# Attention scores: one four-byte matmul against three passes over rounded parts, and one bias load per head against eight

## The reference

```python
s = jnp.einsum('brqhd,brakhd->bhrqak', qg, kg,
               preferred_element_type=jnp.float32) * (d ** -0.5)
bias = rpb[:, dr[:, None, :, None], dc[None, :, None, :]]
s = s + bias[None].astype(jnp.float32)
s = jnp.where(col_in[None, None, None, :, None, :], s, -jnp.inf)
p = jax.nn.softmax(s.reshape(B, H, rows, GRID_W, kr * GRID_W), axis=-1).reshape(s.shape)
o = jnp.einsum('bhrqak,brakhd->brqhd', p.astype(v.dtype), vg)
```

## Time and profile before

| | |
|---|---|
| time, median of 3 runs | 2923.58 us (2922.88 to 2926.93) |
| the profiled execution | 2923.64 us, span from first to last instruction 2922.1 us |
| TensorE busy | 95% of the span |
| VectorE, ScalarE, GpSimd busy | 55%, 45%, 13% |
| mean granted TensorE clock | 0.981 of full speed |

### The profile page before, as it was taken

The page is one execution under the profiler, slowest core; times in us unless marked ns, Lnnn a source line. Parts: engine busy times, 40 slices in busy tenths (PEclk is TensorE's granted clock), DMA queues, the critical chain, the costliest instruction groups (busy, mean ns, idle before and its releaser), DMA issues.

```text
span 2922.1 us, 33578 instructions
## 1 busy us (share of the span) xinstructions
PE 2778.2 (95%) x12738; PEld 2280.3 (78%) x12738; DVE 1599.1 (55%) x1769; ACT 1325.6 (45%) x1459; POOL 388.6 (13%) x603
## 2 busy tenths in 40 slices
PE   8999999999999999989999966999999999999993
PEld 7888888888888887768777745888888888888882
DVE  4111111321333236675234647888888888888885
ACT  6111111211111115654232324777777777777774
POOL 1200000020110033571010101000000000000002
PEclk9999999999999999999999987999999999999996
DMA  8322112121332247534353557999999999999997
GB/s 317 89 79 79 65 57 79 58 100 50 106 103 101 86 146 221 183 105 143 125 173 128 166 172 284 379 401 403 390 400 407 402 404 404 404 400 406 400 394 277
DMA packets 193952, 663.74 MB, mean 227 GB/s; under 512 B 24073, under 2 KB 49176, under 8 KB 170656
## 3 DMA queue, kind: packets, MB, share of 16 engines
q1 hardware_dynamic: 169088, 564.52, 51.3%
q0 software_dynamic: 24736, 97.54, 10.0%
HBM read 588.09 MB, written 73.83 MB: 227 GB/s over the span
## 4 chain that ended last, share of the span: by engine, by line
PE 90%; DMA 2%; DVE 2%; POOL 2%; issue 2%; ACT 1%; SPq 0%; POOLq 0%; DVEq 0%; ACTq 0%
PE ps L2178 24%; PE ps L1877 18%; PE ps L1855 6%; PE ps L1856 6%; PE ps L1857 6%; PE ps L2118 4%; PE ps L2120 4%; PE ps L2119 4%; PE ps L2201 4%; PE ps L2200 4%; PE ps L2199 4%; PE ps L1940 1%; PE ps L1920 1%; PE ps L2157 1%; PE ps L2082 1%
## 5 line engine op out<-in xcount | busy, mean ns | idle before, releaser
L1764 DVE TENSOR_TENSOR elo<-eraw,ehi 128x2048 fp32r<-128x2048 f32 x384 | 874.5, 2292 | 137.0 <-ACT ehi L1223 130.3
L1223 ACT ACTIVATE ehi<-eraw 128x2048 fp32r<-128x2048 f32 x384 | 733.3, 1920 | 250.2 <-PE ps L2178 163.7
L1307 DVE TENSOR_TENSOR wlo<-raw,whi 128x1024 fp32r<-128x1024 f32 x96 | 117.6, 1225 | 705.5 <-ACT whi L969 705.5
L969 ACT ACTIVATE whi<-raw 128x1024 fp32r<-128x1024 f32 x96 | 101.7, 1059 | 733.2 <-PE ps L1877 393.3
L2178 PE MATMUL ps<-elo,xh 128*128 128x512 f32 x960 | 373.8, 389 | 0.0
L2178 PE MATMUL ps<-ehi,xh 128*128 128x512 f32 x960 | 373.7, 389 | 0.0
L1855 PE MATMUL ps<-whi,a_hi 128*128 128x512 f32 x768 | 300.2, 391 | 10.1 <-DVE a_lo L1317 10.1
L1856 PE MATMUL ps<-wlo,a_hi 128*128 128x512 f32 x768 | 300.0, 391 | 0.0
L1857 PE MATMUL ps<-whi,a_lo 128*128 128x512 f32 x768 | 300.0, 391 | 0.0
L2178 PE MATMUL ps<-ehi,xl 128*128 128x512 f32 x960 | 256.7, 389 | 0.0
L1877 PE MATMUL ps<-a_hi,whi 128*128 128x512 f32 x768 | 236.9, 390 | 1.8 <-DVE t L1339 1.6
(11 more groups left out here) (264 smaller groups left out, 3920.4 us busy)
## 6 DMA issues: line engine op xcount, KB each, us to landing
eraw<-in_w_gate SPq DMA_DIRECT2D x256, 512.0 KB, 6.1
eraw<-in_w_up SPq DMA_DIRECT2D x256, 512.0 KB, 8.3
eraw<-in_w_down SPq DMA_DIRECT2D x128, 1024.0 KB, 10.6
raw<-in_w_stream SPq DMA_DIRECT2D x96, 512.0 KB, 3.5
oraw<-in_w_stream SPq DMA_DIRECT2D x128, 256.0 KB, 2.6
scr_rows<-stage POOLq DMA_DIRECT2D x48, 256.0 KB, 2.3
scr_feats<-stage POOLq DMA_DIRECT2D x44, 256.0 KB, 2.3
t<-in_xT SPq DMA_DIRECT2D x16, 512.0 KB, 5.7
```

What stands on the lines that cost most here:

```text
L1223: act.activation(ehi[:, p % ERING, :], flat2(eraw[:, 2 * (p % EDEEP):2 * (p % EDEEP) + 2, :]), ACT.Copy)\
L1764: dve.tensor_tensor(elo[:, p % ERING, :], flat2(eraw[:, 2 * (p % EDEEP):2 * (p % EDEEP) + 2, :]), ehi[:, p % ERING, :].bitcast(F32), ALU.s ...
```

## The change

The scores are made like the projection: ScalarE copies each head's `naq` and `nak` (128x1024 each) into rounded parts, VectorE subtracts these in place, which leaves the remainders where `naq` and `nak` were, and `qk` is three fp32r matmuls of 384 columns into one bank. The copies and subtractions of head `h + 1` stand in the lists of ScalarE (iterations 1 and 2 of head `h`) and VectorE (iterations 2 and 3); those of head 0 stand in the last projection block. `qk` waits for the second remainder (`na_lo`) where it waited for the transfer. Beside it, GpSimd writes a second scratch tensor `rpb_skew` with 8 DMAs from `rpb_rep`, once, behind the store of projection block 7, and `fetch_skew` becomes one DMA of 384 KB.

```diff
             def fetch_skew(h):
 
-                for r in range(QR):
-                    row = h * 15 + 7 - r
-                    sp.dma_start(skew[r * QC:(r + 1) * QC, h % 2, :, :], t["rpb_rep"][:, row:row + 16, :]).then_inc(nbsem[h % 2], 16)
+                sp.dma_start(skew[:, h % 2, :, :], t["rpb_skew"][:, h * 15:h * 15 + 16, :]).then_inc(nbsem[h % 2], 16)
...
+            pool.wait_ge(S["rep_out"], 16 * QC)
+            for r in range(QR):
+                pool.dma_start(t["rpb_skew"][r * QC:(r + 1) * QC, :, :], t["rpb_rep"][:, QR - 1 - r:P - r, :]).then_inc(S["rep_out"], 16)
...
+            def query_high(h):
+
+                hb = h % 2
+                act.wait_ge(nqsem[hb], 32 * (h // 2) + 32)
+                if h >= 2:
+                    act.wait_ge(S["qk_done"], 8 * (h - 1))
+                act.activation(naq_hi[hb][:, :], naq[:, hb, :], ACT.Copy).then_inc(S["na_hi"], 1)
+
+            def key_high(h):
+
+                act.activation(nak_hi[h % 2][:, :], nak[:, h % 2, :], ACT.Copy).then_inc(S["na_hi"], 1)
...
                 evict_pt(v)
                 if v + NAD < NAU:
                     expo(v + NAD)
+                if v % 8 == 1 and v + 8 < NAU:
+                    query_high(v // 8 + 1)
+                if v % 8 == 2 and v + 8 < NAU:
+                    key_high(v // 8 + 1)
...
+            def query_low(h):
+
+                hb = h % 2
+                dve.wait_ge(S["na_hi"], 2 * h + 1)
+                dve.tensor_tensor(naq_lo[hb][:, :], naq[:, hb, :], naq_hi[hb][:, :].bitcast(F32), ALU.subtract).then_inc(S["na_lo"], 1)
...
                 if v:
                     finish(v - 1)
+                if v % 8 == 2 and v + 8 < NAU:
+                    query_low(v // 8 + 1)
+                if v % 8 == 3 and v + 8 < NAU:
+                    key_low(v // 8 + 1)
...
                 if u == 0:
-                    pe.wait_ge(nqsem[hb], 32 * (h // 2) + 32)
+                    pe.wait_ge(S["na_lo"], 2 * h + 2)
...
-                pe.matmul(score_bank(v), q, k, start=True, stop=True).then_inc(S["qk_done"], 1)
+                pe.matmul(score_bank(v), q_hi, k_hi, start=True, stop=False)
+                pe.matmul(score_bank(v), q_hi, k_lo, start=False, stop=False)
+                pe.matmul(score_bank(v), q_lo, k_hi, start=False, stop=True).then_inc(S["qk_done"], 1)
```

More of the change, by code:

```diff
@@ L166, in trunk, with place_split @@
         stage_end, = place(19456, ("stage_end", [P, 4, BW]))
+        def place_split(at, *names):
+            stack = ExitStack()
+            stack.enter_context(nc.sbuf_tensor("below_" + names[0], [P, (at - ROOM) // 4], F32))
+            made = [stack.enter_context(nc.sbuf_tensor(name, [P, SEQ], F32R)) for name in names]
+            stack.close()
+            return made
+        nq0_lo, nq1_lo, nk0_lo, nk1_lo = place_split(126464, "nq0_lo", "nq1_lo", "nk0_lo", "nk1_lo")
+        nq0_hi, nk0_hi = place_split(216576, "nq0_hi", "nk0_hi")
+        nq1_hi, nk1_hi = place_split(118336, "nq1_hi") + place_split(55296, "nk1_hi")
+        naq_lo, nak_lo, naq_hi, nak_hi = (nq0_lo, nq1_lo), (nk0_lo, nk1_lo), (nq0_hi, nq1_hi), (nk0_hi, nk1_hi)
         mv0, mv1, mbc0, kn1, wexp, kw, qkw = place(
@@ L254, in trunk @@
                   "c_updated hs_done ones_done gate_act gate_arg gate_out "
-                  "gates_in h_out0 g_sum wr_in").split():
+                  "gates_in h_out0 g_sum wr_in na_hi na_lo").split():
             S[n] = sem(n)
@@ L268, in trunk @@
         REDO = NE - 2
-        ER0 = [32 * BLK + 16 * OHB * KD // RING] * RING + [32 * (NAH // 2)] * 2 + [256 * (NAH // 2)] * 2 + [128 * (NAH // 2)] * 2
+        ER0 = [32 * BLK + 16 * OHB * KD // RING] * RING + [32 * (NAH // 2)] * 2 + [256 * (NAH // 2)] * 2 + [16 * (NAH // 2)] * 2
         def rows_landed(eng, T):
@@ L509, in fetch_ml_o @@
                 sp.dma_start(mo[h % 2][:, :, :], row_tiles(2048 + h * DV, 2048 + (h + 1) * DV)).then_inc(mosem[h % 2], 16)
-            sp.wait_ge(S["rep_out"], 16 * QC)
+            sp.wait_ge(S["rep_out"], 16 * (QC + QR))
             sp.wait_ge(S["w_used"], 7 * (BLK - 1) + 4)
@@ L768, in _ @@
                 mask_tile(y)
-            pool.wait_ge(nbsem[0], 128)
+            pool.wait_ge(nbsem[0], 16)
             pool.wait_ge(S["nmask_done"], 6)
@@ L786, in _ @@
             for h in range(1, NAH):
-                pool.wait_ge(nbsem[h % 2], 128 * (h // 2 + 1))
+                pool.wait_ge(nbsem[h % 2], 16 * (h // 2 + 1))
                 if h >= 2:
@@ L1037, in _ @@
             feats_high(BLK - 1, True)
+            def query_high(h):
[6 more added lines that the diff above has]
+                act.activation(nak_hi[h % 2][:, :], nak[:, h % 2, :], ACT.Copy).then_inc(S["na_hi"], 1)
+            query_high(0)
+            key_high(0)
             def misc_bank(h, j):
@@ L1450, in feats_low, with key_low @@
                         low(b + 1, m)
+                else:
+                    query_low(0)
+                    key_low(0)
                 evict_feats(b)
+            def query_low(h):
+                hb = h % 2
+                dve.wait_ge(S["na_hi"], 2 * h + 1)
+                dve.tensor_tensor(naq_lo[hb][:, :], naq[:, hb, :], naq_hi[hb][:, :].bitcast(F32), ALU.subtract).then_inc(S["na_lo"], 1)
+            def key_low(h):
+                hb = h % 2
+                dve.wait_ge(S["na_hi"], 2 * h + 2)
+                dve.tensor_tensor(nak_lo[hb][:, :], nak[:, hb, :], nak_hi[hb][:, :].bitcast(F32), ALU.subtract).then_inc(S["na_lo"], 1)
             for b in range(ROWBLK + 2, BLK):
@@ L1914, in qk @@
                 if u == 0:
-                    pe.wait_ge(nqsem[hb], 32 * (h // 2) + 32)
+                    pe.wait_ge(S["na_lo"], 2 * h + 2)
                 if v >= NAD:
                     pe.wait_ge(S["scored"], v - NAD + 1)
-                q = naq[:, hb, u * P:(u + 1) * P]
-                k = nak[:, hb, :].rearrange("p (r c) -> p r c", c=GW)[:, 4 * r:4 * r + WR, KCOL[c]:KCOL[c] + WC]
-                pe.matmul(score_bank(v), q, k, start=True, stop=True).then_inc(S["qk_done"], 1)
+                q_hi, q_lo = (a[hb][:, u * P:(u + 1) * P] for a in (naq_hi, naq_lo))
+                k_hi, k_lo = (a[hb][:, :].rearrange("p (r c) -> p r c", c=GW)[:, 4 * r:4 * r + WR, KCOL[c]:KCOL[c] + WC]
+                              for a in (nak_hi, nak_lo))
+                pe.matmul(score_bank(v), q_hi, k_hi, start=True, stop=False)
+                pe.matmul(score_bank(v), q_hi, k_lo, start=False, stop=False)
+                pe.matmul(score_bank(v), q_lo, k_hi, start=False, stop=True).then_inc(S["qk_done"], 1)
             def tr(v):
@@ L2229 @@
     "m_rows": (8, SEQ), "decays": (8, TT), "q_rows": (2, P, SEQ),
-    "rpb_rep": (QC, P, 48), "h2": (SEQ, D),
+    "rpb_rep": (QC, P, 48), "rpb_skew": (P, P - QR + 1, 48), "h2": (SEQ, D),
 }
```

## The result

| | before | after |
|---|---|---|
| time, median of 7 runs | 2923.58 us (2921.9 to 2926.93) | 2935.03 us (2933.61 to 2937.2) |
| span of the profiled execution | 2922.1 us | 2934.2 us |
| mean granted TensorE clock | 0.981 | 0.980 |

The change makes the kernel slower by 11.4 us: ratio 1.0037, interval 1.0026 to 1.0047. I forecast 2925.4 and no measurable change. The time lies at the upper end of the range, where the rival "slower by transfers" (2934.4) stood.

What follows compares the result with a forecast made beforehand. TensorE was taken to bound an attention iteration of 1.64 us. Passes -7.8, splits +7.0 and transfers +2.6 summed to +1.8 us on 2923.64, giving 2925.4 us, range 2917 to 2935, no measurable change (0.48).

Steps and rivals of the forecast that it cites:

- slower by transfers: Rival: mLSTM bytes land as late as before, heads 5, 6, 7 wait 5.3, 3, 4.5 us, clock falls; 2934.4 us, chance 0.26.
- three passes: Scores on TensorE: three matmuls of 0.173 make 0.52 us instead of 0.65, gaining 7.8 us over 59 iterations.
- splits: Copies on ScalarE and subtractions on VectorE stall TensorE 1.0 us per head, 7.0 us lost over seven heads.
- transfers: Attention stage: `nak` needed four iterations sooner; waits and clock cost 9.2 us against 6.6 now, 2.6 us lost.
- Slower by the passes: Rival: a 384-column matmul on TensorE costs 0.2266 us as 512 columns do; 2932.1 us, chance 0.07.
- The third stall of 0.4: Per head: second subtraction ends late, score and exponential follow late, and `evict_pt` misses its `pv` by about 0.4 us.
- VectorE two subtractions of 1.23 us: Split step: for heads 1 to 7 VectorE gets two subtractions per head of 1.23 us each.
- the 0.7 that I took off for the shorter SyncE list: Head 5's `nak`: landing taken at 1146.5, where the bound by the bytes was 1147.2.
- less 3 us for skew: Head 7's `nak`: the merged skew load brings its landing 3 us sooner, to 1177.3, leaving a wait of 2.4 us.
- The clock: Behind head 5's wait of 4.5 us TensorE's clock falls to its lower level, charged at 1.3 us.
- The rest cost nothing: Head 0's split and GpSimd's `rpb_skew` copy add no time; TensorE would stop only past 33 us of convolution delay.

Runs made afterwards that it cites:

- experiment 6: Changed kernel with the 2 MB of mLSTM loads issued behind `naq` and `nak` of the next head, not ahead of them: 2922.82 us, ratio 0.9994 to the kernel before.
- experiment 5: Changed kernel with GpSimd's bias additions for a head held back until both remainders of that head are written: 2930.39 us, ratio 1.0020 to the kernel before.
- Experiment 2: Changed kernel with the bias change undone, eight skew loads per head and no `rpb_skew`: 2937.2 us, ratio 1.0040 to the kernel before.

## Why the prediction was right and wrong

The number was 9.6 us or 0.33% short, and the case was wrong: I forecast no change, and the kernel is slower by more than the 0.2% that can be told. Of the cases, the rival "slower by transfers" came nearest, with part of its mechanism. That its 2934.4 lies 0.6 us from the 2935.03 is luck: it has 11.6 us for transfers and 7.0 for splits, head 6 waiting for `nak`, and nothing for GpSimd. By the steps of the sum, on the stage:

| step | predicted us | measured us |
|---|---|---|
| three passes | -7.8 | -6.5 |
| splits | +7.0 | +4.2 |
| transfers | 9.2 - 6.6 = +2.6 | 15.3 - 7.0 = +8.3 |
| GpSimd beside VectorE | no term | +7.4 |
| sum | +1.8 | +13.4 |

The measured column is how the stage divides by heads. Taken away one at a time, the place of the loads (experiment 6) makes the stage 11.2 us shorter and the time 13.3, GpSimd's work beside the splits (experiment 5) makes them 8.6 and 5.8 shorter.

**The passes: right, a little smaller.** A matmul of 384 columns costs 0.178 and not 0.173, and an iteration is 0.11 shorter and not 0.13, which leaves 0.54 for the scores if turning and values cost what they did. The starts don't show these 0.54 as such: the first pass now starts 0.25 and not 0.33 after the turning, and from its start to that of the values it is 0.61. "Slower by the passes" is refuted by the rows: 384 columns are cheaper than 512.

**The splits: the mechanism right, the term too large.** The stalls are where I put them, `pv` behind ScalarE's `probT`: 0.2 in iteration 3 of the head and 0.4 in iteration 4. The third stall of 0.4, through VectorE and a late exponential, did not come in heads 1 and 3. 0.6 per head and seven heads make 4.2.

**What failed first: "VectorE two subtractions of 1.23 us".** The duration came from rows of the projection, a stage in which GpSimd adds nothing beside them. In the stage to which they move GpSimd adds bias rows. Four of the fourteen subtractions took 3.69, 1.91, 1.62 and 3.07 us. Two copies of `thr` (128x32) went from 0.18 and 0.19 to 0.97 and 1.05 in head 5, and TensorE waited 1.38 us behind them. In experiment 5 all subtractions are back at 1.21 to 1.23 and both copies at 0.19, and the time is 5.8 us lower. The 7.4 of the table contain the rest of head 0, which still loses 1.7 us more than a clean split with GpSimd out of the way, 1.0 of it perhaps through the wait for the store shown at experiment 5; no run separates it. They also contain 0.3 us in which ScalarE waited for `nak` of head 3.

The page of the Trainium skill "SBUF — State Buffer", section "Who interferes with whom", would have given this step: a VectorE instruction with two SBUF inputs and a GpSimd instruction that reads SBUF exclude each other. The trace agrees for the subtraction, 3.69 us instead of 1.22. The `thr` copies have one input; for copies the same section says that they can contend too, in the modes in which VectorE uses both port pairs. 0.97 and 1.05 us instead of 0.18 and 0.19 agree with that, but no row shows the mode of a copy.

**What failed second: the size of the transfers.** The place (heads 5 and 7) and the carrier (ScalarE's list) were right. The waits of heads 5, 6, 7 and 3 are 6.5, 0, 5.6 and 0.3 us where I had 4.5, 0.5, 2.4 and nothing. For head 5 I had `nak` landing at 1146.5; it let the copy go at 1153.48. 5.2 of that come from `nav` of head 4 starting later, which is mostly head 0's loss passed on; the copy itself was ready 5.0 later too (1146.99 for 1142.0), so this part nearly cancels. The rest is on the transfer's side: from the issue of `mq` to the landing took 14.0 us and 12.8 before, with the same bytes ahead, and why it is 1.1 longer no run shows; and the 0.7 that I took off for the shorter SyncE list did not come. Head 7 shows the same. I took "less 3 us for skew" off the 21.5 us between `nav` of head 6 and the landing; it is 1188.18 - 1165.61 = 22.6. Experiment 2 says directly that the issue does not set it: an issue 2.95 us later did not land later. Experiment 6 gives the price of the bytes' place, 13.3 us of time. It is more than the difference of 8.3 in the table, because it also removes what the kernel before was paying for them, 7.0 on the stage.

**The clock.** A window around head 5's wait has TensorE busy 5.46 of 12 us and a granted clock of 0.77 on average, so it fell for a part to the lower level (1.2 GHz), as I had charged:

```profile
1145.00:1157.00 12.00, 5.46 (x37) 5.13 (x35) 4.82 (x17) 5.00 (x12) 5.77 (x6) 0.77 1.05 316
1176.00:1192.00 16.00, 10.79 (x77) 10.47 (x76) 8.42 (x33) 8.65 (x22) 7.44 (x7) 0.91 1.00 313
```

Head 4 lost 7.8 beyond a clean split with a wait of 6.5: 1.3 on top. No experiment separates the clock from the wait.

**The rest cost nothing: right.** GpSimd's copy held the first convolution output back from 759.42 to 765.96, and TensorE was busy for all 200 us of the window from 600 to 800.

**Open.** The stage grew by 13.4 and the time by 11.4 (span 12.1); the 1.3 us between stage and span were given back later, and I did not look for where. The long subtraction in head 6 (3.07 us for `nk_lo`, beside GpSimd's two multiplications of `qs`, 2.36 and 3.36 us) is counted under transfers. TensorE's wait for it, 1.04 us, is the part that the trace shows; experiment 6, where the transfers are out of the way and TensorE waits 1.7 us for it, says that it would not have gone with them.

## What to carry to other kernels

Before a tensor is split on the engines that feed TensorE, look up where its operands must have landed then, not where they must now: here four iterations sooner, with the small copies that TensorE needs queued behind the waiting one. A duration from another stage holds only if the neighbours are the same; put GpSimd's list beside VectorE's for every two-input operation that moves. And try the order of the DMA list first: with the queue full, moving the loads that are needed last behind those needed next, together with the merged bias load, gave 9.8 us without touching an operation, and the passes on top took 3.1 of it back.

## What the runs showed of the hardware

- Beside GpSimd's additions of two SBUF tiles (six of 128x384 in 5.83 us) a VectorE subtraction of 128x1024 took up to 3.69 us for 1.22, and a VectorE copy of 128x32 0.97 and 1.05 us for 0.18. It was not always held to the end of the row of additions: in head 0 it ended 1.1 us behind that, in head 2 (1.91 us) 0.9 us ahead of it. VectorE's score, which reads PSUM and a bias tile, kept its 0.56. GpSimd lost where the subtraction got in first: up to 2.04 us for an addition of 1.01, 6.81 for six instead of 5.83.
- fp32r matmuls of 384 columns follow each other in 0.178 us in one bank at the higher clock, 512 columns in 0.2266.
- A 512 KB load that landed 4.7 us after its issue in the median took 11.1 and 11.9 us with about 2 MB queued ahead of it.
